# Mixer steps in another place, a first level with 64 standing columns, and single feature tiles of x at the head of a two-layer decoder kernel

## What is computed

```python
z = h @ w_in                       # retention q,k,v,gate and GLA q,k,v,low-rank,gate
ro = retention(rope(rq), rope(rk), rv)          # 4 heads, fixed decay
log_a = log_sigmoid(ga @ w_a2 + b_a2) / 16      # 4 heads, decay per key dimension
# GLA: S_t = diag(a_t) S_(t-1) + k_t^T v_t,  o_t = q_t S_t
out = concat(rmsnorm(ro) * silu(rg), rmsnorm(go) * silu(gg)) @ w_out
```

## Time and profile before

| | |
|---|---|
| median of 3 runs | 1184.18 us (1184.04 to 1184.34) |
| the profiled execution | 1184.15 us |
| its span | 1182.1 us |
| PE busy | 1172.7 us, 99% of the span, 6164 instructions |
| DVE busy | 841.4 us, 71% |
| ACT busy | 702.6 us, 59% |
| POOL busy | 150.4 us, 13% |
| mean granted clock of TensorE | 0.999 of full speed |
| DMA | 217.92 MB, mean 184 GB/s |

### The profile page before, as it was taken

One profiled execution on the slowest core, in us unless ns is written; L12 is line 12 of the kernel. 1 busy time (PEld: TensorE's weight loads), 2 busy tenths in 40 slices (PEclk: granted clock), 3 DMA queues, 4 the chain that ended last, 5 costly groups with the idle time before them and its releaser, 6 DMA issues. The chain is left out here.

```text
span 1182.1 us, 17336 instructions
## 1 busy us (share of the span) xinstructions
PE 1172.7 (99%) x6164; PEld 997.3 (84%) x6164; DVE 841.4 (71%) x1300; ACT 702.6 (59%) x1225; POOL 150.4 (13%) x220
## 2 busy tenths in 40 slices
PE   9999999999999999999999999999999999999998
PEld 7888888788888888888888888887888888888886
DVE  6866656888767678775487875479887676777752
ACT  7655545756666557654476764376567565666641
POOL 3000002573100100000000000036431001000000
PEclk9999999999999999999999999999999999999999
DMA  9756554454545365555465555554545454555540
GB/s 358 271 184 235 194 202 160 175 179 143 195 144 178 131 204 199 178 201 209 142 214 193 198 196 196 196 201 138 179 154 185 144 177 146 202 187 183 201 168 35
DMA packets 33411, 217.92 MB, mean 184 GB/s; under 512 B 3952, under 2 KB 4208, under 8 KB 9792
## 3 DMA queue, kind: packets, MB, share of 16 engines
q1 hardware_dynamic: 33200, 216.90, 53.7%
q10 hardware_dynamic: 144, 0.13, 0.0%
HBM read 215.97 MB, written 1.05 MB: 184 GB/s over the span
## 5 line engine op out<-in xcount | busy, mean ns | idle before, releaser
L1539 DVE SCALAR_TENSOR_TENSOR w_lo<-raw,first,w_hi 128x512 fp32r<-128x512 f32 x576 | 417.2, 779 | 81.4 <-ACT w_hi L1089 80.2
L1089 ACT ACTIVATE w_hi<-raw,first 128x512 fp32r<-128x512 f32 x568 | 369.1, 716 | 90.3 <-PE acc L761 47.0
L760 PE MATMUL acc<-xT,w_hi 128*128 128x512 f32 x864 | 300.2, 391 | 0.0
L761 PE MATMUL acc<-xT,w_lo 128*128 128x256 f32 x864 | 241.9, 280 | 0.0
L585 PE MATMUL acc<-w_hi,xT 128*128 128x512 f32 x576 | 227.4, 395 | 0.0
L589 PE MATMUL acc<-w_lo,xT 128*128 128x512 f32 x576 | 224.6, 390 | 0.7 <-DVE w_lo L1539 0.7
L586 PE MATMUL acc<-w_hi,xT 128*128 128x512 f32 x576 | 224.4, 390 | 0.0
L760 PEld LDWEIGHTS acc<-xT,w_hi 128*128 128x128 f32 x864 | 161.6, 187 | 35.4
L1531 DVE TENSOR_TENSOR w_lo<-raw,w_hi 128x1024 fp32r<-128x1024 f32 x112 | 124.6, 1146 | 87.5 <-ACT w_hi L1083 87.2
L761 PEld LDWEIGHTS acc<-xT,w_lo 128*128 128x128 f32 x864 | 163.3, 189 | 0.1
L1083 ACT ACTIVATE w_hi<-raw 128x1024 fp32r<-128x1024 f32 x112 | 106.6, 991 | 92.2 <-PE acc L589 75.5
(11 more groups left out here) (219 smaller groups left out, 1377.8 us busy)
## 6 DMA issues: line engine op xcount, KB each, us to landing
raw<-in_gu SPq DMA_DIRECT2D x86, 1024.0 KB, 5.1
raw<-in_down SPq DMA_DIRECT2D x32, 1024.0 KB, 4.8
raw<-in_in SPq DMA_DIRECT2D x24, 1024.0 KB, 5.1
raw<-in_kv SPq DMA_DIRECT2D x16, 1024.0 KB, 5.2
raw<-in_down SPq DMA_DIRECT2D x16, 768.0 KB, 4.2
raw<-in_out SPq DMA_DIRECT2D x8, 1024.0 KB, 5.1
raw<-in_q SPq DMA_DIRECT2D x8, 1024.0 KB, 5.1
raw<-in_o SPq DMA_DIRECT2D x8, 1024.0 KB, 5.1
```

The source lines that it names most:

```text
L760: pe.matmul(o[:, :], w_hi[:, slot, kk, c:c + P], xT[:, :, k, :], start=k == 0, stop=False)
L761: mm = pe.matmul(o[:, TOK:2 * TOK], w_lo[:, slot, kk, c:c + P], xT_hi[:, k, :], start=False, stop=k == KD - 1)
L1089: act.activation(w_hi[:, slot, k, :], raw[:, slot, k, :], ACT.Copy, scale=gains[:, ds(g, 1)]).then_inc(s_hi, 1)
L1539: dve.scalar_tensor_tensor(w_lo[:, slot, k, :], raw[:, slot, k, :], gains[:, ds(g, 1)], w_hi[:, slot, k, :].bitcast(F32), ALU.mult, ALU.su ...
```

## The change

Six parts.
1. At the mixer's entry DVE makes two of the four low parts of c1's second half ahead of `x_norm` of the second token tile and two behind it, in place of all four behind; PE's transposes move from tile 5 to tile 6 of that pass.
2. `second_keys` (retention scores and level 0) moves from tile 4 of pass 5 to the end of pass 5, and level 1 from there to tile 4 of pass 6.
3. DVE makes the first two low parts of c3's second half ahead of `retention_mask(1)` and `level_out(0)`.
4. At block size 64 each product has 64 standing columns instead of 128, and DVE copies 64 partitions where it merged 128 under a mask.
5. At the head x's first two feature tiles come alone, the first weights are issued before them, and DVE, not ACT, rounds the first tile. SP's queue has one DMA more.
6. The warm-up has 9 products instead of 12.

```diff
@@ -154,9 +154,9 @@
 POOL_STEPS = 38
-WARM = 12
+WARM = 9
 FIRST = ((0, 0, 1), (0, 1, 2), (0, 2, 3), (0, 3, 4), (1, 0, 2), (1, 2, 4))
-XT_IN = ((0, 2), (2, 4), (4, 6), (6, 8))
+XT_IN = ((0, 1), (1, 2), (2, 4), (4, 6), (6, 8))
 
@@ -299,6 +299,7 @@
         s_xt = [sem(f"x_by_feature_loaded{i}") for i in range(len(XT_IN))]
+        s_x0 = sem("first_x_tile_step")
         s_ones = sem("ones_ready")
@@ -502,15 +503,16 @@
                              src[:, k0 * COL:k1 * COL]).then_inc(s_piece[n], 16)
+            first_weights(0)
             first_xt(0)
-            first_weights(0)
+            first_xt(1)
             first_weights(1)
-            first_xt(1)
+            first_xt(2)
             first_weights(2)
             first_weights(3)
-            first_xt(2)
+            first_xt(3)
             first_weights(4)
-            first_xt(3)
+            first_xt(4)
             first_weights(5)
@@ -719,7 +721,9 @@
                             pe.wait_ge(s_hi, ks + 1)
-                            if k % 2 == 0:
+                            if ks == 0:
+                                pe.wait_ge(s_x0, 2)
+                            elif ks == 1 or k % 2 == 0:
                                 pe.wait_ge(s_tev, ks // 2 + 1)
@@ -834,7 +838,8 @@
                             c = c0 + (2 * t + r) * 64
-                            mm = pe.matmul(mb[e][:, c:c + 64], tile, later, start=True, stop=True)
+                            keys = 64 if b == 64 else P
+                            mm = pe.matmul(mb[e][0:keys, c:c + 64], tile[:, 0:keys], later, start=True, stop=True)
                             if last and t == TT - 1 and r == 1:
@@ -940,7 +945,7 @@
                 def second_tile(ks):
-                    if ks == 5:
+                    if ks == 6:
                         x_transposes(l, 1, 1)
@@ -949,9 +954,9 @@
                     level(l, 0, False, True)
-                inside = {4: {4: gqk_transposes}, 5: {4: second_keys}, 7: {4: lambda: levels(l, 2)},
+                inside = {4: {4: gqk_transposes}, 6: {4: lambda: level(l, 1, True, True)}, 7: {4: lambda: levels(l, 2)},
                           8: {4: lambda: levels(l, 4)}, 9: {4: lambda: levels(l, 6)}, 10: {4: retention_outputs}}
-                behind = {4: lambda: retention_scores(0), 5: lambda: level(l, 1, True, True), 10: gated_outputs,
+                behind = {4: lambda: retention_scores(0), 5: second_keys, 10: gated_outputs,
                           11: lambda: mixed_transposes(l, 0)}
@@ -1477,8 +1482,8 @@
                 act.wait_ge(s_xt[n], 16)
-                k = n % 2 * 2
-                act.activation(xT_hi[:, 2 * n:2 * n + 2, :], by_feature[n // 2][:, k:k + 2, :],
+                k0, k1 = XT_IN[n]
+                act.activation(xT_hi[:, k0:k1, :], by_feature[k0 // 4][:, k0 % 4:k0 % 4 + k1 - k0, :],
                                ACT.Copy).then_inc(s_thi, 1)
@@ -1488,16 +1493,16 @@
                                    scale=gains[:, g:g + 1]).then_inc(s_hi, 1)
-            first_x(0)
             act.wait_ge(s_first, 16)
             first_weights(0)
+            first_x(1)
             first_weights(1)
-            first_x(1)
+            first_x(2)
             first_weights(2)
             first_weights(3)
-            first_x(2)
+            first_x(3)
             first_weights(4)
-            first_x(3)
+            first_x(4)
             first_weights(5)
@@ -1766,6 +1771,9 @@
                         src = mb[e][:, c0:c0 + 4 * 64].rearrange("p (c g b) -> p c g b", c=4, b=b)
+                        if b == 64:
+                            dve.tensor_copy(dst[0:64, :, 0, :], src[0:64, :, 0, :]).then_inc(s_mf[e], 1)
+                            continue
                         msk = lv_mask[:, n - 1, :].rearrange("p (g b) -> p g b", b=b)
@@ -1809,8 +1817,9 @@
 
+                split_lo(l, C_IN + 1, 1, ks=(0, 1))
                 x_norm(l, 1, 1)
-                split_lo(l, C_IN + 1, 1)
+                split_lo(l, C_IN + 1, 1, ks=(2, 3))
                 x_lo(l, 1, 1)
@@ -1854,9 +1863,10 @@
                                       ALU.mult).then_inc(s_pg, 1)
+                split_lo(l, C_IN + 3, 1, ks=(0, 1))
                 retention_mask(1)
                 level_out(0)
-                split_after(4)
+                split_lo(l, C_IN + 3, 1, ks=(2, 3))
                 level_out(1)
@@ -2042,18 +2052,23 @@
             def first_x(n):
-                dve.wait_ge(s_thi, n + 1)
-                k = n % 2 * 2
-                p = (slice(None), slice(2 * n, 2 * n + 2), slice(None))
-                dve.tensor_tensor(xT_lo[p], by_feature[n // 2][:, k:k + 2, :], xT_hi[p].bitcast(F32),
-                                  ALU.subtract).then_inc(s_tev, 1)
-            first_x(0)
-            split_lo(0, 0, 0, ks=(0, 1))
+                dve.wait_ge(s_thi, n)
+                k0, k1 = XT_IN[n]
+                dve.tensor_tensor(xT_lo[:, k0:k1, :], by_feature[k0 // 4][:, k0 % 4:k0 % 4 + k1 - k0, :],
+                                  xT_hi[:, k0:k1, :].bitcast(F32), ALU.subtract).then_inc(s_tev, 1)
+            dve.wait_ge(s_xt[0], 16)
+            dve.tensor_copy(xT_hi[:, 0:1, :], by_feature[0][:, 0:1, :]).then_inc(s_x0, 1)
+            dve.wait_ge(s_x0, 1)
+            dve.tensor_tensor(xT_lo[:, 0:1, :], by_feature[0][:, 0:1, :], xT_hi[:, 0:1, :].bitcast(F32),
+                              ALU.subtract).then_inc(s_x0, 1)
+            split_lo(0, 0, 0, ks=(0,))
             first_x(1)
+            split_lo(0, 0, 0, ks=(1,))
+            first_x(2)
             split_lo(0, 0, 0, ks=(2, 3))
-            first_x(2)
+            first_x(3)
             split_lo(0, 0, 1, ks=(0, 1))
-            first_x(3)
+            first_x(4)
             split_lo(0, 0, 1, ks=(2, 3))
```

## The result

The changed kernel takes 1192.81 us (1190.71 to 1193.35, six runs), the kernel before beside it 1184.26 us (1184.04 to 1184.71): a ratio of 1.0068, with an interval of 1.0055 to 1.0081. It is slower by 8.6 us where 2.9 us of gain were forecast. The profiled execution took 1193.35 us with a span of 1191.2.

The account below looks back on a forecast made before the run. PE, busy 99% of the span, was taken as the bound, so only its stops could yield gain: 1184.15 - 1.22 (entry) - 1.66 (levels 0 and 1) = 1181.3 us, with head and 64 columns at 0; range 1180.6 to 1182.9.

Parts of the forecast that it names:

- 64 standing columns: Level 1's sixteen matmuls: gain between nothing and 0.45 us, booked at 0 because PE meets POOL at level 5; DVE's copy 0.
- Rival 3: Level 1 waits for DVE's two low parts, each held by a whole POOL instruction: 0.9 us lost per layer, 1183.1; chance 0.05.
- Rival 4: Clock rise missed after the shorter warm-up; slower only if four of the first eight tiles run so, 5.4 us lost; chance 0.04.
- The sign that I named for the head: Matmuls of the first chunk starting 0.45 us apart would show the forecast wrong.
- The entry: Mixer's entry: two low parts ahead of x_norm remove PE's stop, gaining 0.68 + 0.54 = 1.2 us; bounds 0.9 and 1.2.
- Levels 0 and 1: PE's stall at level 0 goes; gain limited where PE meets POOL at level 5, 0.83 us per layer, 1.66 in all.
- rival 1: The stall moves to level 5, by level 4's tie to ACT or DVE-POOL slowing: gain 0.1 per layer, 1182.7; chance 0.13.
- Head: Kernel start: first matmul 0.1 to 0.4 us earlier, tile 2 as before at 9.26; booked 0, bounds +0.5 and -0.3.
- Rival 2: Head is late: tile 2's weights land one issue later, costing 0.45 us, 1181.8; chance 0.14.
- my sign of 9.5: At the head, tile 2 starting past 9.5 us would show the forecast wrong; it was expected near 9.26.

Follow-up runs that it names:

- experiment 1: The change with DVE's masked merge of level 1 over 128 partitions put back, 64 standing columns kept: 1183.16 us against 1183.91 for the kernel before.
- experiment 4: The kernel before with only the 64 standing columns and DVE's plain 64-partition copy added: 1190.84 us, ratio 1.0060.
- experiment 5: The change with the plain copy of level 1 replaced by a masked merge over the same 64 partitions: 1192.53 us, single execution.
- experiment 6: The change with a plain copy over 128 partitions and 128 standing columns at the level of 64: 1182.78 us, single execution.
- experiment 2: The change with both 128 standing columns and the masked merge over 128 partitions put back: 1183.33 us, ratio 0.9993.
- experiment 3: The change with DVE waiting for POOL's operand of level 2 before its run of eight low parts: 1188.08 us, ratio 1.0037.
- the head alone: The kernel before with only the change's head (input pieces, issue order, first tiles, shorter warm-up): 1184.73 us, ratio 1.0004.
- experiment 13: The change with the masked merge of 128 partitions and the old head, so the mixer's parts alone: 1183.06 us, ratio 0.9992.
- experiment 16: The change with the 128-partition masked merge, old head, levels 2 and 3 one tile later, levels 4 and 5 two: 1180.27 us, ratio 0.9968.
- experiment 10: The change with level 1's copy replaced by masked merges over partitions 0 to 63, then 64 to 127: 1183.89 us.
- experiment 17: The version of experiment 16 with 128 standing columns and the 128-partition masked merge at the level of 64: 1180.82 us, ratio 0.9972.
- experiment 18: The version of experiment 16 with the change's new head in place of the old one: 1180.60 us, ratio 0.9970.

## Why the prediction was wrong

**The step that failed** is half a sentence under "64 standing columns": "DVE's copy in place of the masked merge is on an engine with slack; 0." The time of the copy is indeed nothing (0.74 us for two, the merge 0.78). What I did not cost is what it does to the taking of turns between DVE and POOL: a hold-off of POOL for the whole run of eight, 4.9 us more than such an instruction needs, in each layer. By the medians it is worth 9.6 us. In the profiled executions, PE waits 6.35 us for POOL (levels 2 and 3) where experiment 1 waits 1.75 (levels 3 and 5), and loses 5.7 us to the lower clock, together 10.3; their times differ by 1193.35 - 1183.02 = 10.3. Experiments 1 and 4 show the cause from both sides, experiments 1 and 5 that the partitions are what counts in it. Without this step the change would still have missed its forecast of 1181.3, by 1.9 us (experiment 1).

**Rival 3 was near.** It had low parts and POOL's instructions blocking each other wholly, but with DVE as the one that waits, at 1.1 us for each of POOL's instructions, and I gave it 0.05 since the rows showed turns of 1.17 us. The rule of the Trainium skill that I weighed there (SBUF — State Buffer, section Who interferes with whom), that a DVE instruction with two SBUF inputs contends with a GpSimd one that reads SBUF, holds in this trace in a harder form than the turns that I read from the rows: one POOL instruction waited for eight of DVE's. Of VectorE's two-port modes the page says that whoever issues first has the shared pair for its instruction; that one side passes eight times is not in what it says, and is measured here (6.07 us, and 3.44 with four). Neither does it name the partitions, on which it hung in experiments 5 and 6.

**Rival 4, the clock**, was right in kind and wrong in place. I looked for it at the warm-up, where the clock rose as before. It fell instead behind new waits of 1.2 to 1.8 us in the middle, which no case of mine had, and nearly doubled their price. The sign that I named for the head does show in two other profiles: in experiments 2 and 3 matmuls of the first tile stand 0.43 us apart. Their transposes start at 202.03 and 201.88 all the same, among the earliest, so it reached nothing behind.

**The entry**, 1.2 us. The mechanism was right: low parts in time, transposes 3 matmuls later in the work at the same moment, no wait. But PE's gain there is not the kernel's: alone it measured 0.1, less than can be told from nothing, because POOL's chain starts 0.5 us earlier and takes 0.4 to 0.5 us longer. I followed POOL's chain for the gain at the levels and not for that at the entry, though both end at the same place, and I had no price for moving two of DVE's low parts beside one of POOL's exponents. The bounds of 0.9 to 1.2 left that out.

**Levels 0 and 1**, 0.83 per layer. The stop at level 0 went, and level 1 came without a wait, as worked out. Where POOL comes back I had 0.12 of slack and POOL 0.71 earlier. In experiment 1 POOL's operand of level 4 starts at 245.54, 0.51 earlier, and that of level 5 is ready 0.43 earlier, while PE, with entry and columns, arrives at level 4 1.29 us earlier (250.18 against 251.47). POOL has no idle time ahead of level 4's operand any more, as I said; but from 226.23 on it has none at all, and its own steps up to there take some 0.4 us longer than before. It could not follow PE further. So level 3 waits 0.24 us, level 5 0.65, and from the transposes to level 6 the first layer gains 0.10 us beyond the three matmuls that now stand ahead of them. That is rival 1, at its price of 0.1 per layer: 1182.7 was its number, and experiment 1, which is the change without the 64-partition copy, took 1183.16. Of its two mechanisms it is not the tie to ACT, but in part the other, DVE and POOL slowing each other in the new order. I gave it 0.13 and the forecast 0.57.

**64 columns**, booked at 0 with a bound of 0.45 per layer. PE gains 0.43 us, the upper bound; sixteen times the 53 ns named there would have been 0.85 us, and 27 ns each were measured. The gain turned into waiting in part, as the text said: 1183.16 with them and 1183.33 without, 1.8 and 1.3 us of waits for POOL. Where nothing waits for POOL any more the medians show some 0.5 us for both layers.

**Head**, booked at 0 with +0.5 as a bound. All comparisons lie on the plus side, none beyond its interval: 0.6 by the median of the head alone, 0.2 to 0.3 in the last comparison. By the start of the transposes the head alone is 0.6 late, but over all profiles the mean is 202.4 with the new head (14) and 202.15 with the old one (6), with the spread told above. Rival 2 had 0.45, from tile 2. That tile starts at 9.41 in the changed kernel, but at 9.92 in the head alone, past my sign of 9.5, behind stops at the tiles before it: the first matmul comes early, and the short stops give that back.

## What to carry to other kernels

Where VectorE and GpSimd both run long series of instructions on SBUF, the order in which they take turns is a resource of its own: look at the longest instruction of each line beside its mean, and do not count a VectorE instruction as free for its duration alone when it changes the partitions it works on. When a stall is removed, follow the engine that released it up to the next meeting with it; if what it delivers does not come earlier, the gain stops there, and moving the consumers later in PE's work (here by one and two tiles; 2.8 us, from experiment 13 to 16, of the 3.9 gained in all) is the change that pays. A wait of PE can bring the clock down behind it, and that is to be costed with it as a chance: in the changed kernel it cost nearly the same amount again, while behind one wait of 2.20 us (experiment 3) and two of 1.0 us (experiment 10) the granted clock stayed at 1.00.

## What the runs showed that I had not expected

- A VectorE instruction on partitions 0 to 63 or 0 to 95, ahead of a run of low parts with two SBUF inputs each, let that run pass POOL's instruction entirely: 6.1 us for eight, 3.4 for four, against 0.7 to 1.2 us with 128 partitions. The low parts ran at 0.67 us each then, against 0.99 to 1.1 in turns. So VectorE is faster for it: the held-off version costs the kernel only because PE waits for POOL.
- The clock did not do the same behind waits of equal length. Behind 1.94 us in experiment 4 it stays at 1.00 in the first layer and falls to 0.50 in the second. Level 5 of experiment 1 waits 0.65 us and the clock stays at 1.00 in the next 6 us; in experiment 2 it waits 0.63 and the windows read

```profile
252.00:254.00 2.00, 2.00 (x18) 1.65 (x17) 2.00 (x3) 0.32 (x1) 2.00 (x3) 0.74 0.93 254
254.00:256.00 2.00, 2.00 (x6) 1.60 (x5) 2.00 (x4) 0.32 (x1) 2.00 (x2) 0.50 0.64 270
256.00:258.00 2.00, 2.00 (x9) 1.63 (x8) 0.82 (x4) 0.60 (x1) 1.78 (x3) 0.91 0.78 188
```

  and from level 5 to the next levels it needs 8.29 us where experiment 1 needs 6.72: 1.6 us. The second layer of the same execution waits 0.65 us and needs 6.72. The eleven times of experiment 13, which has the same wait, lie at 1182.45 to 1183.13 (eight) and 1184.49 to 1184.89 (three), and its profiled execution, one of the three, shows the fall in the first layer. So behind a wait of 0.6 us PE can lose another 1.6 us; that this makes the two groups of times is likely but seen in one profile only. The versions without the wait show no second group that far apart: their times lie within 0.5 us (experiment 16), 1.0 (17) and 1.2 (18).
